# A two-network transformer kernel: a first slice of the constants loaded ahead, another order behind the last solve slot, and output tiles dealt over the attention tails

## The reference

```python
# first network, each layer: ffn; then
h = rms_norm(x, mix_norm[layer]);  p = h @ w_in            # gates, sgu, rwkv inputs
y_a = chunked_sgu(...)                                     # 1024 channels
y_b, v_first = rwkv7_time_mix(...)                         # a scan, then group norm, + bonus
merged = sigmoid(gate_a) * (y_a @ w_proj_a) + sigmoid(gate_b) * (y_b @ w_proj_b)
x = x + merged @ w_out                                     # then another ffn
# second network, each layer: ffn; then
y = fox_attention(h, ...)  or  dilated_attention(h, ...)   # 16 heads; o @ w_out at the end
x = x + gate * y                                           # then another ffn
```

## Time and profile before

| | us |
|---|---|
| median of 3 executions | 2909.57 (2904.04 to 2914.23) |
| the profiled execution | 2906.58 |
| its span, first to last instruction | 2904.9 |
| TensorE busy / VectorE busy / ScalarE busy | 2798.3 / 2116.2 / 1569.7 |

### The profile page before, as it was taken

How to read it: one execution, slowest core, us unless ns; L and a number is a source line. 1 busy time by engine, 2 the same in 40 slices (tenths; PEclk the granted TensorE clock), 3 DMA queues, 4 the chain that set the end, 5 groups by cost and what they waited for, 6 DMA issues and landing times.

```text
span 2904.9 us, 53242 instructions
## 1 busy us (share of the span) xinstructions
PE 2798.3 (96%) x22460; PEld 2498.3 (86%) x22460; DVE 2116.2 (73%) x3137; ACT 1569.7 (54%) x2364; POOL 13.2 (0%) x23
## 2 busy tenths in 40 slices
PE   7999999989999999999999899998999999998999
PEld 6889888888888898888888788887888879998888
DVE  6877667668778777666688687566878876776765
ACT  5545644346555455444465455465555646675653
POOL 0000000000000000000000000000000000000000
PEclk9999999999999999999999999899999999999999
DMA  6674311246756743112467467432675664332454
GB/s 225 249 284 179 117 45 46 89 146 236 270 214 249 280 178 111 60 46 89 147 230 259 165 236 268 165 123 95 248 264 202 260 237 160 146 131 102 147 187 145
DMA packets 72765, 510.61 MB, mean 176 GB/s; under 512 B 8464, under 2 KB 9104, under 8 KB 11728
## 3 DMA queue, kind: packets, MB, share of 16 engines
q1 hardware_dynamic: 72528, 507.21, 48.0%
HBM read 506.13 MB, written 1.05 MB: 175 GB/s over the span
## 4 chain that ended last, share of the span: by engine, by line
PE 85%; DVE 9%; ACT 4%; issue 2%; DMA 1%; SPq 0%; ACTq 0%; DVEq 0%
PE solve_banks L2058 13%; PE solve_banks L2114 10%; PE linear_banks L2058 7%; PE solve_banks L2059 7%; PE solve_banks L2115 5%; PE linear_banks L1956 5%; PE linear_banks L1957 4%; PE linear_banks L1958 4%; PE linear_banks L2059 4%; PE linear_banks L2502 3%; PE linear_banks L2503 3%; PE linear_banks L2504 3%; DVE split_halves L1301 2%; PE solve_banks L2365 1%; PE solve_banks L2074 1%
## 5 line engine op out<-in xcount | busy, mean ns | idle before, releaser
L1301 DVE TENSOR_TENSOR split_halves<-raw_units,split_halves 128x1024 fp32r<-128x1024 f32 x806 | 973.0, 1222 | 362.3 <-ACT split_halves L908 359.7
L908 ACT ACTIVATE split_halves<-raw_units 128x1024 fp32r<-128x1024 f32 x806 | 842.8, 1054 | 459.6 <-PE solve_banks L2115 197.2
L2058 PE MATMUL solve_banks<-h_split,split_halves 128*128 128x512 f32 x1680 | 589.2, 395 | 3.1 <-DVE split_halves L1301 3.1
L2114 PE MATMUL solve_banks<-hidden_split,split_halves 128*128 128x512 f32 x1408 | 491.9, 393 | 0.0
L2059 PE MATMUL solve_banks<-h_split,split_halves 128*128 128x256 f32 x1680 | 469.0, 279 | 0.0
L2115 PE MATMUL solve_banks<-hidden_split,split_halves 128*128 128x256 f32 x1408 | 393.6, 280 | 0.0
L2058 PEld LDWEIGHTS solve_banks<-h_split,split_halves 128*128 128x128 f32 x1680 | 315.0, 188 | 77.7 <-DVE split_halves L1301 2.2
L2058 PE MATMUL linear_banks<-h_split,split_halves 128*128 128x512 f32 x912 | 323.6, 397 | 5.7 <-DVE h_split L1371 4.0
L2059 PEld LDWEIGHTS solve_banks<-h_split,split_halves 128*128 128x128 f32 x1680 | 316.6, 188 | 0.0
L2114 PEld LDWEIGHTS solve_banks<-hidden_split,split_halves 128*128 128x128 f32 x1408 | 264.3, 188 | 58.3
L1956 PE MATMUL linear_banks<-h_split,split_halves 128*128 128x256 f32 x864 | 263.2, 305 | 5.4 <-DVE split_halves L1301 4.5
(11 more groups left out here) (329 smaller groups left out, 4881.5 us busy)
## 6 DMA issues: line engine op xcount, KB each, us to landing
raw_units<-in_stream SPq DMA_DIRECT2D x403, 1024.0 KB, 4.8
raw_units<-in_mod_w SPq DMA_DIRECT2D x72, 1024.0 KB, 6.1
x<-in_x SPq DMA_DIRECT2D x4, 256.0 KB, 4.4
w2a<-in_w2a SPq DMA_DIRECT2D x2, 512.0 KB, 6.1
w_rows<-in_w SPq DMA_DIRECT2D x2, 512.0 KB, 7.5
bs_rows<-in_bs SPq DMA_DIRECT2D x2, 512.0 KB, 8.6
spatial_t<-in_ws_t SPq DMA_DIRECT2D x2, 512.0 KB, 10.8
out<-x SPq DMA_DIRECT2D x4, 256.0 KB, 4.1
```

The costliest lines, as they stand in the source:

```text
L908: nc.scalar.activation(split[:, n % SPLIT_SLOTS, 0, :], raw[:, item % RAW_SLOTS, (n % 2) * HALF * P:(n % 2 + 1) * HALF * P], ACT.Copy).the ...
L1301: V.tensor_tensor(split[:, n % SPLIT_SLOTS, 1, :], raw[:, item % RAW_SLOTS, (n % 2) * HALF * P:(n % 2 + 1) * HALF * P], split[:, n % SPLIT ...
L2058: M(pairs(banks[:, e, :]), s[:, 0, t], h[:, :, k, :], start=k == 0, stop=False)
L2114: M(pairs(bank), s[:, 0, t], hidden[:, :, k, :], start=k == 0, stop=False)
```

## The change

1. The constants are laid out anew, with the matrix of means and the small biases first (131 of 866 columns; one column, `final_eps`, is new and unused). These 131 columns are loaded by a transfer of their own behind `columns`; the rest comes after weight unit 2. The first waits are for the small part, a later one is for the rest.
2. Behind the last solve slot: on VectorE the product of pa 2 moves ahead of the variance, and the splits are spread singly between the norm's steps; ScalarE splits further ahead; in each pb slot the gate product moves ahead of the splits; pa 2 is emptied before the variance's bank in the plan.
3. The value transposes of layer 0 go two behind pb 1, one behind pb 2, one behind pb 3.
4. The fills of the attention tails are a table (`FILLS`): smaller pieces, reaching channel tile 7 (halves 0 and 1) or 6 (halves 2 and 3), dealt between the tasks. Each further fill step also spreads the tasks behind it: in both layers tasks 13 to 15 now have fills between their steps.

```diff
-for _name, _n in (("ident", P), ("mean", P), ("head", P), ("tri", 129), ("mask", 2 * P), ("ident_sub", SUB), ("slide", 30), ("norm_eps", 1), ("ln_eps", 1)):
+for _name, _n in (("mean", P), ("norm_eps", 1), ("ln_eps", 1), ("final_eps", 1), ("ident", P), ("head", P), ("tri", 129),
+                  ("mask", 2 * P), ("ident_sub", SUB), ("slide", 30)):
...
+VALUES_BACK = ((), (0, 1), (2,), (3,))
...
-FILL_K = (4, 6)
+FILLS = ({26: ((0, 0, 4),), 27: ((1, 0, 4),), 28: ((2, 0, 4),), 29: ((3, 0, 4),), 30: ((0, 4, 6),), 31: ((1, 4, 6),),
+          32: ((2, 4, 6), (3, 4, 6)), 33: ((0, 6, 7), (1, 6, 7))},
+         {72: ((0, 0, 6),), 73: ((1, 0, 6),), 74: ((2, 0, 2),), 75: ((2, 2, 4),), 76: ((2, 4, 6), (3, 0, 4)),
+          77: ((3, 4, 6),), 78: ((0, 6, 7), (1, 6, 7))})
+FILLED_TO = (7, 7, 6, 6)
...
-        elif half < halves + 4:
-            steps.append(("fill", half - halves))
+        elif half in FILLS[l]:
+            steps.append(("fill", half))
...
+                    sp.dma_start(const[:, 0:FIRST_CONSTS], src["const"][:, 0:FIRST_CONSTS]).then_inc(mean_loaded, 16)
...
-            load(1)
-            sp.dma_start(const[:], src["const"]).then_inc(consts_loaded, 16)
-            load(RAW_SLOTS - 1)
+            load(RAW_SLOTS)
+            sp.dma_start(const[:, FIRST_CONSTS:], src["const"][:, FIRST_CONSTS:]).then_inc(consts_loaded, 16)
...
                 group_norm("square", l, 3)
-                keep_ahead(proj + 4)
+                keep_ahead(proj + 6)
                 group_norm("root", l, 3)
-                keep_ahead(proj + 6)
+                keep_ahead(proj + 8)
                 group_norm("high", l, 3)
...
                 group_norm("mean", l, 3)
                 keep_ahead(proj + 4)
+                first_product(l, 2)
                 for stage in ("var", "invert0", "invert1", "invert2", "invert3"):
                     group_norm(stage, l, 3)
-                first_product(l, 2)
+                keep_ahead(proj + 5)
+                group_norm("scale", l, 3)
                 keep_ahead(proj + 6)
-                for stage in ("scale", "affine", "bonus"):
-                    group_norm(stage, l, 3)
+                group_norm("affine", l, 3)
+                group_norm("bonus", l, 3)
+                keep_ahead(proj + 7)
+                group_norm("rest", l, 3)
                 keep_ahead(proj + 8)
-                group_norm("rest", l, 3)
                 first_product(l, 3)
                 for s in range(4):
-                    keep_ahead(proj + 8 + 2 * s + 1)
                     w = slice(2 * s, 2 * s + 2)
                     bank = wait_filled(dve, ("pb", l, s))
                     V.tensor_tensor(diff[:], pairs(bank), gate_sig[:, 1, w, :], ALU.mult).then_inc(emptied["dve"], 1)
+                    keep_ahead(proj + 8 + 2 * s + 1)
...
-                if l == 0:
-                    pe.wait_ge(yb_temp, 4)
-                    for s in range(4):
-                        transposes(("vback", l, s), v_)
-                for s in (2, 3):
-                    two_tiles(proj + 8 + 2 * s, ("pb", l, s), (YB, YB))
+                pe.wait_ge(yb_temp, 4)
+                for s in range(1, 4):
+                    if s > 1:
+                        two_tiles(proj + 8 + 2 * s, ("pb", l, s), (YB, YB))
+                    for m in VALUES_BACK[s] if l == 0 else ():
+                        transposes(("vback", l, m), v_)
```

More of the change, by code:

```diff
@@ L68 @@
 NCONST = _at
+FIRST_CONSTS = CONST["ident"][0]
 FIRST_HALF = ("score0", "score1", "seed", "z0", "p0", "z1", "p1", "z2", "p2", "z3", "p3")
@@ L332, in make_plan @@
         p.use(("gmean", l, 3), "dve")
-        p.use(("pa", l, 2), "dve", at_once=False)
-        p.fill(("pa", l, 2))
+        p.use(("pa", l, 2), "dve")
         p.use(("gvar", l, 3), "dve")
-        p.empty(("pa", l, 2))
         p.use(("pa", l, 3), "dve")
@@ L339, in make_plan @@
             p.use(("pb", l, s), "dve")
-            if l == 0 and s == 1:
-                for m in range(4):
-                    p.use(("vback", l, m), "act")
+            for m in VALUES_BACK[s] if l == 0 else ():
+                p.use(("vback", l, m), "act")
         p.stream(("out", l), 4)
@@ L546, in build_program @@
     cols_loaded = signal("cols_loaded")
+    mean_loaded = signal("mean_loaded")
     c_loaded = signal("c_loaded")
@@ L1128, in rwkv @@
                         .then_inc(merged_hi, 1)
-                    if l == 0 and s == 1:
-                        for m in range(4):
-                            bank = wait_filled(act, ("vback", l, m))
-                            nc.scalar.activation(v_first[:, 2 * m:2 * m + 2, :], pairs(bank), ACT.Copy)\
-                                .then_inc(emptied["act"], 1)
+                    for m in VALUES_BACK[s] if l == 0 else ():
+                        bank = wait_filled(act, ("vback", l, m))
+                        nc.scalar.activation(v_first[:, 2 * m:2 * m + 2, :], pairs(bank), ACT.Copy)\
+                            .then_inc(emptied["act"], 1)
                 for d in range(4):
@@ L1198, in attention @@
                         keep_ahead(base + n)
-                    elif step == "fill" and n == 0:
+                    elif step == "fill" and n == 2 * len(TILES[l]):
                         keep_ahead(out + 3, 0)
@@ L1271, in _ @@
                 norm_square(0, i)
-            act.wait_ge(consts_loaded, 16)
+            act.wait_ge(mean_loaded, 16)
             for l in range(2):
@@ L2025, in first_tiles @@
                         if n == 0 and k == 4:
-                            pe.wait_ge(consts_loaded, 16)
+                            pe.wait_ge(mean_loaded, 16)
                         if k == 4:
@@ L2140, in rwkv @@
                                   h_wait(3 * l + 1) if s == EARLY_UNITS else None)
+                pe.wait_ge(consts_loaded, 16)
                 pe.wait_ge(small_loaded, 80 * (l + 1))
@@ L2433, in attention @@
                     elif step == "fill":
-                        part_of_out(l, n, 0, FILL_K[l])
+                        for part in FILLS[l][n]:
+                            part_of_out(l, *part)
                     elif step == "decay":
@@ L2467, in attention @@
                     if d < 2:
-                        part_of_out(l, 2 * d, FILL_K[l], DT)
-                        part_of_out(l, 2 * d + 1, FILL_K[l], DT)
+                        for n in (2 * d, 2 * d + 1):
+                            part_of_out(l, n, FILLED_TO[n], DT)
                     else:
@@ L2586, in constants @@
     put("ln_eps", LN_EPS)
+    put("final_eps", NORM_EPS ** 2)
     levels = np.zeros((2, SUB, len(LEVELS), 2, SUB), np.float32)
```

## The result

| | us |
|---|---|
| changed kernel, median of 20 executions | 2892.3 (2885.69 to 2908.44) |
| kernel before, median of 20, same chip | 2909.57 (2903.37 to 2918.24) |
| ratio | 0.9943, interval 0.9932 to 0.9955 |
| profiled execution of the changed kernel, its span | 2902.05, 2900.3 |

The change wins 17.3 us; forecast were 17.1 and a time of 2892. The profiled execution lies some 10 us above the median.

The account below looks back on a forecast made before the run. TensorE was taken as the bound, leaving only its idle time and low-clock stretches to win. Layer 0 6.7, layer 1 3.2, fox 3.6, dilated 4.0, less 0.4 at the start, gave 17.1 us: 2892, range 2883 to 2903.

Parts of the forecast that it names:

- The bound: Whole kernel: TensorE busy 2798.3 of 2904.9 us; only its idle time and lower-clock stretches can be won.
- Layer 0, first half: Behind layer 0's last solve slot, up to pb 1's end: waits of 1.41 and 1.64 us go.
- Layer 0, second half: From pb 1's end to the output: 1.8 us idle before pb 2, 1.3 before output; whole stretch wins 6.7.
- Layer 1: Behind layer 1's last solve slot: waits 0.25, 0.9 and 2.0, idle 3.15 instead of 6.39 us, 3.2 won.
- Fox tail: End of fox attention and output work: last o 1.4 us earlier, 5.0 together, 1.4 charged for clock, 3.6 won.
- Dilated tail: End of dilated attention: last o 4.3 us earlier, output work 5.3 instead of 6.74, 1.7 charged for clock, 4.0 won.
- The start: Kernel start: ScalarE's wait for weight unit 0 grows, costing 0.4 us, with ends 0 and 0.9.
- The sum: Whole kernel: 6.7 + 3.2 + 3.6 + 4.0 - 0.4 = 17.1 us won.
- Clock stays low in the tails: Rival, attention tails: the clock stays low and their gains vanish, 9.5 us won, 2900; chance 0.12.
- Splits late: Rival, behind the solve slots: splits come late, layer 0 keeps 3 us, layer 1 nothing, 2899; chance 0.10.
- Full clock everywhere: Rival, both tails: denser work holds TensorE at 2.4 GHz, 25.4 us won at most, 2884; chance 0.09.
- Whole turn exposed: Rival, eight pb slots: TensorE waits out VectorE's whole turn of 5.2 us in each, slower at 2928; chance 0.04.

Follow-up runs that it names:

- e10: The changed kernel itself, unaltered, run once more on another chip: 2894.6 us against 2912.03 for the kernel before, ratio 0.9931.
- e5_order: The changed kernel with the split ahead of the gate product in each pb slot again: 2897.43 us against 2914.55 for the kernel before.
- e3: The kernel before with only the table of fills for the attention tails added: 2906.0 us against 2911.63, ratio 0.9983.
- e8: Changed kernel with last pb slot's splits and pb 1's gate product earlier, first squares' sums two output halves later: 2884.79 us against 2914.55 for the kernel before.
- e11: The kernel of e8 again, on the chip of e10: 2884.27 us against 2912.03 for the kernel before, ratio 0.9908.

## Why the prediction was right, point by point

**The bound.** TensorE's idle time and its clock, nothing else: right. The same work stands in both profiles. Layer 0, layer 1 and the fox tail shortened mostly by their waits (4.7, 3.1 and 2.4 of 5.8, 3.4 and 3.0), the dilated tail by its clock.

**Layer 0, first half (no waits).** Right, with nothing to spare. H10 was forecast 4.1 behind the end of pa 3 and was split 4.09 behind it (587.92 less 583.83). TensorE reached it after 4.1, not 4.4: its first matmul on H10 stands at 587.97, and the timeline reports no wait there.

**Layer 0, second half (1.8 and 1.3).** The waits are 2.26 and 1.71. The chain is right: forecast from pa 3's end to the second gate product's end 14.9, measured 598.44 less 583.83 = 14.6. The term mis-sized is TensorE's own way to it, 13.1 forecast and 12.4 measured: the four halves of pb 0 and 1 took 11.5 instead of 11.9, the eight transposes 0.9 instead of 1.2. A faster TensorE waits longer for the same chain. The stretch gained 5.7 in the profile and 7.2 in e10 (36.00 less 28.81); forecast 6.7. Between the two lies pb 2's clock, 1.5. The upper end of 8.7 was meant for "nothing idles and the clock stays full", but by the prediction's own 26.1 that is 9.9 (36.00 less 26.1); 8.7 leaves the clock out.

**Layer 1 (0.25, 0.9, 2.0).** Measured 0.59, 0.57, 2.12, in sum 3.28 for 3.15; gain 3.37, 3.2 forecast.

**Fox tail (3.6).** Counted from the last split ahead of the tail, TensorE goes on behind the last o after 27.22 (1988.97 less 1961.75) instead of 28.67 (1985.38 less 1956.71): 1.45 earlier, 1.4 forecast. With 3.6 for the output work that made 5.0 before the charge for the clock. That 3.6 was too high: from the last o to the second pair's first matmul it took 6.41 (1988.97 to 1995.38), so 2.5 less than the 8.90 before. The terms listed in the prediction for it add to 5.55 at full clock and 6.15 at half, not to 5.3. e5_order, with the same fills, gained 4.7, so nearly that; the changed kernel 3.0. The difference between the two is the clock's, 1.7 where I charged 1.4. First the changed kernel, then e5_order, each the 4.90 up to the first squares' sums and the 5.13 behind:

```profile
1988.97:1993.87 4.90, 4.18 (x18) 3.89 (x19) 2.73 (x4) 3.66 (x6) 0.00 (x0) 0.50 0.01 3
1993.87:1999.00 5.13, 5.13 (x21) 4.77 (x22) 4.34 (x8) 1.80 (x4) 0.00 (x0) 0.54 0.55 204
```
```profile
1984.42:1989.32 4.90, 3.71 (x18) 3.51 (x18) 2.73 (x4) 3.66 (x6) 0.00 (x0) 0.69 0.01 3
1989.32:1994.45 5.13, 5.13 (x40) 5.03 (x41) 4.35 (x8) 2.88 (x6) 0.00 (x0) 1.00 0.55 206
```

Behind the squares that is 21 matmuls against 40 in the same time. The runs with these fills fall into two groups, -2.7 to -3.2 and -4.7 to -5.0, and my 3.6 was the value of neither. In the first group the clock of the stretch is 0.95; in the second it is 0.98 in e3 and e5, and 0.97 with 0.7 less idle time in e8 and e11, which have the sums later.

**Dilated tail (4.0).** In its first profile, nearly right in number: the last o was forecast 4.3 earlier; its output work starts after 29.37 (2691.20 less 2661.83) instead of 33.52 (2692.56 less 2659.04), 4.15 earlier. The prediction got there by filled waits and a clock back at full for half of the time. Some waits shrank (4.11 to 1.80, and two of 1.11 to 0.41), but others grew (0.89 to 1.77, the one for the squares 1.29 to 2.52) or are new (1.07 at 2672.49). So the idle time of the whole stretch fell only from 12.30 to 11.85, and the clock did the rest (0.98 for 0.89). In e10, with the same waits to 0.2, the output work starts only 1.6 earlier than in the kernel before. So the number owes much to the clock of that execution. From there to the second pair, 6.74 fell to 5.68 (2691.20 to 2696.88), 5.3 forecast. The charge of 1.7 for the clock was not paid in the profile: from 2671.42 on it stood at 1.00, and the stretch gained 5.2. In e10 the clock took more than that (1.1 gained). Of nine profiles with these fills seven gain 4.8 to 5.4, so here I charged too much as a rule; two unchanged tails already lie 1.0 and 1.3 under the kernel before's.

**The start (+0.4).** +0.32 in the profile, not told apart from the spread of 0.6.

**The sum.** 5.8 + 3.4 + 3.0 + 5.2 less 0.3 is 17.1 in the profile's stretches, by the sum's own terms: layer 0 0.9 too high, fox 0.6 too high, dilated 1.2 too low, and they cancel. In e10, the same kernel, the same sum is 14.7, while the medians there differ by 17.4. The medians' 17.3, with an interval of some 13 to 20, bears out the total, not each term, and that it agrees to 0.2 is luck. The clock takes part in it: on the chip of e10 the changed kernel's executions have mean granted clocks of 0.985 to 0.990, those of the kernel before 0.981 to 0.986.

**The rivals.** *Clock stays low in the tails*: falls as a rule, but holds for single tails of single executions. *Splits late*: H10 was at its edge, no more. *Full clock everywhere*: it had the direction for the dilated tail only. The Trainium skill's "TensorE: Matmul & The Clock Gate", Part 1, has activity release the throttle. The trace does not bear that out for this short stretch: ahead of the squares both tails hold the same 18 matmuls in 4.90 us, yet the clock is 0.50 in the fox tail (TensorE busy for 4.18) and 1.00 in the dilated tail (busy for 2.38, 2691.20 to 2696.10). What differs is the level that it had on arriving. *Whole turn exposed*: no; a gate product is missed only before pb 2 of layer 0, and splits in the three places that the count gave.

**Not settled:** what decides between the two levels in one and the same program; whether the new fills raise the clock of the dilated tail, as eight of nine profiles suggest, and if so by the dealing or by channel tile 7.

## What to carry to other kernels

When an engine in order both empties banks and prepares operands, write down for each place which of the two TensorE misses first. The better order differed from slot to slot here (gate product first in the slots of pb 0 to 2, split first in that of pb 3), and one rule for all slots left 4.0 us of idle time lying. Short filler work (here 16 transposes) that needs banks is best dealt one or two banks at a time between long uses. Filler matmuls dealt into a chain of softmaxes in short pieces cut its longest wait (4.11 to 1.8) and the fox tail's idle time by 2.4; that they gain time in the dilated tail at an equal clock isn't shown. Before a few us are explained by a change, run the same kernel twice, compare stages, and read each stage's idle time and clock apart.

## What the runs showed of the hardware that was not expected

- TensorE's clock differs between executions of one program, at fixed places: 1.00 or 0.66 at 291 to 306 us, and from 0.92 down to 0.50 at 1098 to 1113, with TensorE busy for 14.31 to 15.00 of 15.00 either way. These two low stretches cost the profiled execution 4.7 and 5.6 us against the kernel before, counted between the splits 90 to 105 and 300 to 310. That is the size of the 10 us by which it lies over the median; e11_best's profile has both low stretches too (4.9 and 5.7) and lies 10.0 over its own. Among the changed kernel's twenty executions, the seven with a mean granted clock of 0.985 or 0.986 took 2894.67 to 2908.44, the thirteen with 0.988 or 0.989 took 2885.69 to 2895.80.
- A low level held past a tail takes back what fewer waits had won: the fox tail gained 3.0 with 0.54 behind it (1993.87 to 1999.00), and 4.7 with 1.00 there.
- Between equal stretches at full clock the chip repeats to 0.2 us of 75 (layer 1: 75.09 to 75.22 in four profiles without the new order). Elsewhere two profiles move against each other by 1 to 3 us within some tens of us, with no edit there; the two places above are the largest found.
